# A gMLP layer's U and output products with the tokens stationary, its mixing by token, and DMA transposes for the blocks

## What is computed

```python
def gmlp_chunk_mixer(h, w_in, ln_g, ln_b, w_s, b_s, w_out):
    z = jax.nn.gelu(h @ w_in)
    u, v = jnp.split(z, 2, axis=-1)
    v = layer_norm(v, ln_g, ln_b)
    vc = v.reshape(B, S // CHUNK, CHUNK, GMLP_GROUPS, GMLP_GROUP)
    ws = jnp.where(causal[None], w_s, 0).astype(v.dtype)
    mixed = jnp.einsum('gts,bnsgc->bntgc', ws, vc) + b_s.T[None, None, :, :, None]
    return (u * mixed.reshape(B, S, GMLP_WIDTH)) @ w_out

def conv_ffn(h, w_gate, w_up, conv_w, conv_b, w_down):
    g = causal_dwconv3(h @ w_gate) + conv_b
    return (jax.nn.silu(g) * (h @ w_up)) @ w_down

for i in range(2):
    h = h + mixer_i(rms_norm(h, ...))
    h = h + conv_ffn(rms_norm(h, ffn_ln[i]), ...)
return rms_norm(h, final_ln)
```

## Time and profile before

| | us |
|---|---|
| median of 3 runs (2198.03 to 2200.35) | 2198.29 |
| span of the profiled execution | 2196.6 |
| PE busy | 2187.2 (100%) |
| DVE busy | 1473.7 (67%) |
| ACT busy | 1152.3 (52%) |
| POOL busy | 62.0 (3%) |
| chain that ended last | PE 99% |
| U, from its first matmul to that of the output product | 94.52 to 190.63 |
| output product | 190.63 to 279.40 |
| F0 | 279.40 to 758.63 |

### The profile page before, as it was taken

How to read it: one execution, slowest core, us unless ns; L and a number is a source line. 1 busy time by engine, 2 the same in 40 slices (tenths; PEclk the granted TensorE clock), 3 DMA queues, 4 the chain that set the end, 5 groups by cost and what they waited for, 6 DMA issues and landing times.

```text
span 2196.6 us, 30226 instructions
## 1 busy us (share of the span) xinstructions
PE 2187.2 (100%) x10468; PEld 1845.2 (84%) x10468; DVE 1473.7 (67%) x1865; ACT 1152.3 (52%) x1476; POOL 62.0 (3%) x56
## 2 busy tenths in 40 slices
PE   9999999999999999999999999999999999999998
PEld 7888888888888888888888888888888888888887
DVE  7486757777776755555468888785767676775554
ACT  7554555555555544444456555555555555554443
POOL 0011100000000000001000000020000000000000
PEclk9999999999999999999999999999999999999999
DMA  7755567777777765555555656558776777786665
GB/s 280 250 174 172 191 208 220 213 220 213 223 214 219 213 201 196 190 188 204 192 184 182 201 180 196 170 185 218 213 223 209 225 209 221 214 243 204 201 199 165
DMA packets 243077, 451.55 MB, mean 206 GB/s; under 512 B 139888, under 2 KB 140016, under 8 KB 242352
## 3 DMA queue, kind: packets, MB, share of 16 engines
q1 hardware_dynamic: 231664, 442.28, 64.5%
q0 software_dynamic: 944, 6.03, 0.8%
q10 hardware_dynamic: 10384, 2.11, 0.5%
HBM read 419.38 MB, written 2.10 MB: 192 GB/s over the span
## 4 chain that ended last, share of the span: by engine, by line
PE 99%; DMA 0%; ACT 0%; DVE 0%; SPq 0%; ACTq 0%; issue 0%
PE acc L1535 25%; PE acc L1537 25%; PE acc L1536 25%; PE acc L1513 14%; PE acc L1514 8%; PE sc_ps L1535 0%; PE sc_ps L1537 0%; PE sc_ps L1536 0%; PE sc_ps L1755 0%; DMA raw<-w_stream 0%; PE acc L1845 0%; PE acc L1663 0%; PE acc L1661 0%; PE acc L1662 0%; PE misc L1786 0%; PE sc_ps L1786 0%
## 5 line engine op out<-in xcount | busy, mean ns | idle before, releaser
L1039 DVE TENSOR_TENSOR w_lo<-raw,w_hi 128x1024 fp32r<-128x1024 f32 x782 | 962.9, 1234 | 612.3 <-ACT w_hi L655 611.3
L655 ACT ACTIVATE w_hi<-raw 128x1024 fp32r<-128x1024 f32 x782 | 828.6, 1062 | 730.3 <-PE acc L1537 603.4
L1535 PE MATMUL acc<-w_hi,X 128*128 128x512 f32 x1688 | 658.1, 390 | 0.0
L1537 PE MATMUL acc<-w_lo,X 128*128 128x512 f32 x1688 | 657.4, 389 | 0.0
L1536 PE MATMUL acc<-w_hi,X 128*128 128x512 f32 x1688 | 657.2, 389 | 0.0
L1537 PEld LDWEIGHTS acc<-w_lo,X 128*128 128x128 f32 x1688 | 317.0, 188 | 65.8
L1536 PEld LDWEIGHTS acc<-w_hi,X 128*128 128x128 f32 x1688 | 317.0, 188 | 65.5
L1535 PEld LDWEIGHTS acc<-w_hi,X 128*128 128x128 f32 x1688 | 317.0, 188 | 65.3
L1513 PE MATMUL acc<-X,w_hi 128*128 128x512 f32 x1024 | 359.2, 393 | 0.0
L1514 PE MATMUL acc<-X,w_lo 128*128 128x256 f32 x1024 | 288.7, 282 | 0.0
L1535 PE MATMUL acc<-w_hi,hid 128*128 128x512 f32 x688 | 268.1, 390 | 0.0
(11 more groups left out here) (211 smaller groups left out, 1350.6 us busy)
## 6 DMA issues: line engine op xcount, KB each, us to landing
raw<-w_stream SPq DMA_DIRECT2D x782, 512.0 KB, 3.9
h<-x_t SPq DMA_DIRECT2D x8, 256.0 KB, 6.1
out<-Z SPq DMA_DIRECT2D x4, 512.0 KB, 3.0
f_turned_a<-hc SPq DMA_TRANSPOSE x88, 3.2
f_turned_a<-tsum SPq DMA_TRANSPOSE x88, 3.2
std_rinv<-hc SPq DMA_TRANSPOSE x88, 4.1
std_rinv<-tsum SPq DMA_TRANSPOSE x88, 3.6
raw<-w_stream SPq DMA_DIRECT2D x4, 256.0 KB, 3.9
```

Source lines behind the costliest of these rows:

```text
L655: nc.scalar.activation(placed(w_hi, slot, exact(c, rounds)), raw[slot][:, :], ACT.Copy).then_inc(hi_ready, 1)
L1039: nc.vector.tensor_tensor(placed(w_lo, slot, at), raw[slot][:, :], placed(w_hi, slot, at), ALU.subtract)\
L1535: nc.tensor.matmul(bank, xh, hi, start=(kt == 0), stop=False)
L1537: op = nc.tensor.matmul(bank, xh, lo, start=False, stop=(kt == k_tiles - 1))
```

## The change

- **U and the output product** use `token_unit`, in blocks of 512 features, eight units each. The output product's units go in the order `AO_SPLIT`: six of block 0, four of block 1, the rest of 0, the rest of 1, then blocks 2 and 3. Weights are laid out to match; `by_depth` goes.
- **U's result**: ACT takes the gelu straight out of PSUM with the token's scale (`u_evac`), for a block at step 8, 16, 24 and 32.
- **Mixing** is done with `WS` stationary and both chunks of V as 256 columns: one matmul a group, four groups behind units 12, 16, 21 and 28. DVE adds the bias and multiplies with U in one instruction a group (`gate`). POOL has no part in it.
- **Turning**: U x mixed, the output product and D0's first three blocks have tokens on the partitions and are turned as F0 turns its results, in one helper: DVE cuts two planes (`cut_rows`), SP issues four DMA transposes of 128x4x128 (`turn_rows`), DVE puts the halves together (`set_rows`). For U the steps of cutting and setting are `U_CUT_AT` and `U_SET_AT`; in the products setting comes two steps after cutting (`SET_AFTER`), the addition to `h` one step later, `x_low` one and two steps after that. The output product and D0 are cut straight from PSUM. D0's last block is still turned on PE.
- `mean_square(0)` and its root and reciprocal go. `token_mean_square(1)` comes one unit later.

```diff
+MIX_AT = {12: 0, 16: 1, 21: 2, 28: 3}
+U_GATE_AT = (16, 19, 25, 32)
+U_CUT_AT = (17, 21, 26, 32)
+U_SET_AT = (20, 24, 29, 34)
+AO_SPLIT = ((0, range(6)), (1, range(4)), (0, range(6, 8)), (1, range(4, 8)), (2, range(8)), (3, range(8)))
+AO_ORDER = [(c, n) for c, ns in AO_SPLIT for n in ns]
+AO_DONE = [1 + max(u for u, (b, _) in enumerate(AO_ORDER) if b == c) for c in range(BLOCKS)]
+SET_AFTER = 2
...
 @block.sync
+            def turn_rows(n):
+                for r in range(2):
+                    sp.wait_ge(row_cut, 2 * n + r + 1)
+                    wait_pos(sp, row_set, 2 * n)
+                    for t in range(2):
+                        sp.dma_start(row_planes[r][:, :, P * t:P * (t + 1)],
+                                     turned_planes[r][:, t, :].rearrange("p (g f) -> p g f", g=4),
+                                     transpose=True).then_inc(row_landed, 16)
...
+            ahead = AHEAD + RING
+            at = loads_and_turns(OPENING, [(R_U + c, U_U + U_CUT_AT[c] + ahead) for c in range(BLOCKS)] +
+                                 [(R_AO + c, U_AO + AO_DONE[c] + ahead) for c in range(BLOCKS)])
...
 @block.gpsimd
-            for j in range(KT // 2 - 1):
-                pool.wait_ge(gelued, P_U + j + 1)
-                pool.wait_ge(mix_ready, 2 * j + 2)
-                nc.gpsimd.tensor_tensor(by_chunk(U[:, 2 * j:2 * j + 2, :]), by_chunk(U[:, 2 * j:2 * j + 2, :]),
-                                        mixed_pair(j), ALU.mult).then_inc(gated, 1)
...
 @block.scalar
+            def u_evac(c):
+                act.wait_ge(units_done, U_U + BLOCK_UNITS * (c + 1))
+                act.wait_ge(tok_rinv_ready, 1)
+                for t in range(2):
+                    nc.scalar.activation(U[:, t, COLS * c:COLS * (c + 1)], acc[c % 2][:, t, :], ACT.Gelu_apprx_tanh,
+                                         scale=tok_rinv[:, t:t + 1]).then_inc(gelued, 1)
+            def gx_high(c):
+                act.wait_ge(row_set, 2 * (R_U + c + 1))
+                act.wait_ge(v_normed, 2 * BLOCKS)
+                for b in range(2):
+                    nc.scalar.activation(GX[:, pair_of(2 * c + b), 0:S], feats_of(R_U + c)[:, pair_of(b), :], ACT.Copy)\
+                        .then_inc(gx_hi, 1)
...
             for k in range(4, KT * KT // UT + 4):
                 split_step(U_U, k)
-                gelu_evac(P_U + j, j, k % 4, j % 2, U, U_U + 4 * (j + 1))
+                if k % BLOCK_UNITS == 0:
+                    u_evac(k // BLOCK_UNITS - 1)
+                if k in U_SET_AT:
+                    gx_high(U_SET_AT.index(k))
...
+            for s in range(4, BLOCKS * BLOCK_UNITS + 4):
                 split_step(U_AO, s)
+                for c in range(BLOCKS):
+                    at = s - AO_DONE[c] - SET_AFTER - 1
+                    if at in (0, 1):
+                        residual(1, P_AO + 2 * c + at, 2 * c + at)
...
 @block.vector
+            def cut_rows(n, source):
+                if n:
+                    dve.wait_ge(row_landed, ROW_TURNS * n)
+                for r in range(2):
+                    nc.vector.tensor_copy(turned_planes[r], source(r)).then_inc(row_cut, 1)
+            def set_rows(n):
+                dve.wait_ge(row_landed, ROW_TURNS * (n + 1))
+                for r in range(2):
+                    nc.vector.tensor_copy(feats_plane(n, r), row_planes[r]).then_inc(row_set, 1)
+            def product_rows(norm, n, pd, c, done, k):
+                if k == 0:
+                    dve.wait_ge(units_done, done)
+                    cut_rows(n, lambda r: acc_plane(c % 2, r))
+                if k == SET_AFTER:
+                    set_rows(n)
+                if k == SET_AFTER + 1:
+                    add_rows(n, pd, c)
+                if k - SET_AFTER - 2 in (0, 1):
+                    pr = 2 * c + k - SET_AFTER - 2
+                    dve.wait_ge(pair_summed, pd + pr + 1)
+                    x_low(norm, pr)
...
+            def gate(c):
+                dve.wait_ge(mixed, c + 1)
+                dve.wait_ge(gelued, 2 * (c + 1))
+                for g in range(4 * c, 4 * (c + 1)):
+                    at = U[:, :, P * g:P * (g + 1)]
+                    nc.vector.scalar_tensor_tensor(at, mix_of(g), ws_bias[:, g:g + 1], at, ALU.add, ALU.mult)\
+                        .then_inc(gated, 1)
...
 @block.tensor
-                    wait_pos(pe, pair_summed, P_U + k // 4 - 1)
-                multiply(U_U + k, k % RING, tiles_of(k // 4 % 2, X, KT, k % 4))
+                token_unit(U_U + k, k % RING, acc[c % 2], X, 2 * n, KT)
+                if k in MIX_AT:
+                    mix(MIX_AT[k])
...
-            product(U_AO, P_AO, KT // 2, GX, KT, gx_needed, deep=True)
+            for k, (c, n) in enumerate(AO_ORDER):
+                if n == 0 and c < 2:
+                    pe.wait_ge(gelued, 2 * (c + 3))
+                elif n == 0:
+                    pe.wait_ge(row_cut, 2 * (R_AO + c - 1))
+                token_unit(U_AO + k, k % RING, acc[c % 2], GX, 2 * n, KT, gx_needed if c == 0 else None)
```

More of the change, by code:

```diff
@@ L261, in trunk @@
         WS = place("WS", at, [P, KT, P])
-        BS = place("BS", at + 8 * BLK, [P, KT, P])
+        row_feats = [place(f"row_feats{i}", at + (8 + 4 * i) * BLK, [P, 4, S]) for i in range(2)]
         v_junk = place("v_junk", 2 * KT * BLK, [P, D // 2])
@@ L283, in trunk @@
         at += 4 * SC * 4
-        down_tok = [nc.alloc_sbuf_tensor_at(f"down_tok{i}", [P, 2, COLS], F32, offset=x_at + (12 + 2 * i) * row)
-                    for i in range(2)] + [place("down_tok2", at - 4 * SC * 4, [P, 2, COLS])]
+        down_tok = place("down_tok", at - 4 * SC * 4, [P, 2, COLS])
+        down_feats = [nc.alloc_sbuf_tensor_at(f"down_feats{i}", [P, 4, S], F32, offset=x_at + (12 + 2 * i) * row)
+                      for i in range(2)]
         nmax = place("nmax", at, [P, 2])
@@ L538, in turn_head, with loads_and_turns @@
                                  transpose=True).then_inc(p_landed[h_ % 2], 16)
+            def turn_rows(n):
[6 more added lines that the diff above has]
+                                     transpose=True).then_inc(row_landed, 16)
+            def loads_and_turns(at, turns):
+                for n, u in turns:
+                    if at < (u + 1) // RING * RING:
+                        loads(at, (u + 1) // RING * RING)
+                    for v in range((u + 1) // RING * RING, u + 1):
+                        next_unit(v)
+                    turn_rows(n)
+                    at = -(-(u + 1) // RING) * RING
+                    for v in range(u + 1, at):
+                        next_unit(v)
+                return at
             def f_block(layer, u0, b):
@@ L660, in settled @@
                 act.wait_ge(vecs_landed, 16)
-            def high_copy(pair, s, done):
-                act.wait_ge(units_done, done)
-                nc.scalar.activation(hc[:, :, :], acc[s][:, :, 0:S], ACT.Copy).then_inc(hcopied, 1)
             def square_pair(n, pr):
@@ L1614, in f_block @@
             def f_block(layer, u0, b, i=0, before=None):
-                if before is None:
+                if before is not None and layer == 0:
+                    pe.wait_ge(row_cut, 2 * (R_AO + 3 + b))
+                elif before is None:
                     pe.wait_ge(f_evacuated, 4 * i + (F_CUTS * layer + 2 * (b - 1)))
@@ L1623, in f_block @@
                                normed_ready(1 + 2 * layer) if before is not None and b == 0 else None, kind=u0)
-                    if before is not None and b == 0 and n == 5:
+                    if before is not None and b == 0 and n == 6 - layer:
                         token_mean_square(1 + 2 * layer, lambda t: ssum[:, P * t:P * (t + 1)])
@@ L1904, in stream @@
     first = by_tokens(w_in[KT:]).reshape(BLOCKS, BLOCK_UNITS, UT, P, P)
[L1905 removed]
+    u_half = by_tokens(w_in[:KT])
+    w_out = by_tokens(blocks(a_w_out)).reshape(BLOCKS, BLOCK_UNITS, UT, P, P)
+    parts = [np.stack([first[c, n] for c, n in V_ORDER]), u_half, np.stack([w_out[c, n] for c, n in AO_ORDER]), by_tokens(ffn[0].reshape(-1, KT, P, P)), by_tokens(blocks(down[0])),
              v[:-1], qk.reshape(-1, P, E), v[-1:], blocks(b_w_o), by_tokens(ffn[1].reshape(-1, KT, P, P)), by_tokens(blocks(down[1]))]
```

289 lines of the change are left out of this document (113 added, 176 removed).

## The result

The changed kernel takes 2201.14 us (median of 21 runs, 2199.83 to 2204.06) against 2198.48 for the kernel before (21 runs beside them): a ratio of 1.0013, 95% interval 1.0007 to 1.0019. It is slightly slower, by 2.7 us, where 2.5 us faster was forecast, and lies just above the range. The profiled execution spans 2199.4 us; the median stands 1.7 us above it, as before.

The account below looks back on a forecast made before the run. PE was taken to set the time, by its own work and by late split units. 7.0 us less PE work minus 4.5 of stalls gave 2.5 us faster, 2195.8 us; range 2191.0 to 2201.0.

Parts of the forecast that it names:

- PE's own work, 7.0 us: PE saves 3.5 by the token form, 2.7 by 24 fewer transposes, 0.4 by one mean square, 0.4 by mixing.
- the form: U and output product: token form takes 2.720 us a unit against 2.774, saving 3.5 us over 64 units.
- mixing: U: 16 mixing matmuls of 256 columns replace 32 of 128 columns, saving 0.4 us on PE.
- the mean square: One mean square on PE goes, saving 0.4 us.
- The cut from PSUM: DVE's copy from PSUM, absent from the earlier trace: bounds 0.68 and 1.23 us, taken as 1.2.
- The landing: The last of a turn's four DMA transposes lands 2.5 us after its own start.
- the rival of late landing: Transposes share DMA engines with weights and land at 4.1 us; stalls 12.1, time 2203.4 us; chance 0.15.
- a landing over 3: Sign of being wrong: a turn's last transpose landing more than 3 us behind its start.
- The stalls, 4.5 us: PE waits for split units behind turns: 1.6 us at place A plus 2.9 at place B.
- Place A: End of U: the turn of its last block makes PE stand 1.6 us before the output product's unit 5.
- Place B: Output product: block 1's turn meets block 0's; PE waits 1.2 us at unit 21, 1.7 at unit 22, 2.9 together.
- Elsewhere nothing: Turns that come alone, F0's unit 6 (X wanted at 16.3, ready at 15.6) and U's blocks 0 to 2: no PE wait.

Follow-up runs that it names:

- e2: Changed kernel without the four DMA transposes of each turn; rows are set from the cut planes unturned, all other work stays: 2191.23 us, ratio 0.9968.
- e1: Kernel before, with only D0's first three blocks turned by DMA transposes: 2195.87 us against 2198.53, ratio 0.9989.
- e8: Changed kernel with POOL's additions of the squares behind the output product cut from 512 columns to 2: 2199.0 us, ratio 1.0003.
- e4: Changed kernel with U's last block set two steps later and the output product's first two blocks ended after 10 and 16 units: 2197.6 us, ratio 0.9996.
- e9: Changed kernel with U's last block set two steps later and output product blocks 0 to 2 set three steps behind their cut: 2191.73 us, ratio 0.9971.
- e11: Changed kernel with only output product blocks 0 to 2 set three steps after their cut instead of two: 2197.02 us, ratio 0.9992.
- e12: Changed kernel with SP's four transposes of U's last block moved ahead of two loads: 2202.83 us, ratio 1.002.
- e7: Changed kernel with one more DMA transpose in each of the 11 turns, into a spare buffer: 2212.14 us, ratio 1.0062.
- e10: e9 with the output product's last block turned on PE instead of by DMA: 2192.21 us, ratio 0.9973.

## Why the prediction was wrong

**What bounds the kernel** held: PE by its own work, and by split units that come late.

**PE's own work, 7.0 us: right, term by term.** e2, without any wait, has a span 6.9 below that of before. The output product falls from 88.77 to 87.04, which is the 32 x 0.054 forecast, and in both stages together the form is worth what F0's rate said. D0 alone gives 2.6 of 2.7 (e1). The output product starts 188.28 - 190.63 = 2.35 earlier; 1.7 of form, 0.4 of mixing and 0.4 of the mean square make 2.5, less 0.2 by which this profile's opening is longer (its first mean square starts at 42.10 instead of 41.91).

**The cut from PSUM: right.** 1.22 us from `acc` against 0.69 from U, both in 16-bit elements. The value taken from the fp32 row of the trace was the right one of the two. The Trainium skill ("VectorE: DVE Perf Modes", "Why PSUM operands drop a tier") caps a copy with an operand in PSUM at the one-port double mode, and the prediction read from this that a 16-bit copy could keep 0.68. But the same page ("Mode 2×_1P — pack two bf16 into one 32-bit read") gives that mode only to 16-bit elements at a step of one, and `acc_plane` takes every second 16-bit half. So the page too has the single mode here, and the trace agrees with it.

**The landing: right as a median, 2.5 us, and late where it counted once.** In nine of the eleven turns the last transpose landed 2.5 us behind its start, in place A too, so the rival of late landing doesn't explain places A and B. In two it landed late: 4.0 in U's block 1, where three steps cover it, and 3.7 in the output product's block 3, where it is half of F0's wait. The prediction named a landing over 3 as a sign of being wrong, and there it is.

**The stalls, 4.5 us: wrong, 9.5.** Three of its steps failed, and one term was missing.

1. *Place A, 1.6; it was 3.4.* The step "First cut: 4.05. Fourth transpose starts at 7.75, lands at 10.25" took 1.23 for each of four issues. The first pair took 3.80: 1.3 us, and the earlier trace rows had the row with the warning, a maximum of 2322 ns. The other 0.4 is DVE's late start at the gates, a split of the step before.
2. *Place B, 2.9; it was 3.7.* The chain was right within 0.3 us at each point, but the split was priced at 1.23 throughout (1.64 beside POOL's addition), ACT's 0.68 us wait between two pairs was left out, and unit 19, late by 0.2 on paper, was counted as nothing. With the first two gone (e8) 2.6 are left. The explanation that went with it, two turns that meet, was not the cause (e4): a lone turn empties the lead, and what follows it wins nothing back. The lead lasts where the set comes one step later (e9, e11), because DVE no longer stands in it, or because block 1's cut then no longer stands behind block 0's low parts; which of the two gives how much is open.
3. *"Elsewhere nothing": unit 31 0.2, F0 2.0.* For F0's unit 6 the sum had 0.7 us to spare, with the engines taken as on time. DVE came with three splits of debt (1.0), the last transpose landed 1.2 later than taken, and the wait was 1.55. In e11, without the debt and with a landing of 2.5, there is none. The token mean square waited for POOL's last sum, another 0.4. A margin below 1 us behind a stage that stalls is no margin.
4. *Missing: a first matmul behind a wait* takes 0.50 us instead of 0.39 to finish, and its successor starts 0.33 behind it instead of 0.23: 0.1 us for each of six waits, included in the numbers above.

The stalls add up: 3.4 + 3.7 + 0.2 + 0.2 (not resolved) in the output product and 2.0 in F0 are 9.5; less 7.0, and with the opening's 0.2, that is 2.7 of the 2.8 measured.

What was not weighed at all is the clock. In the changed kernel's profile it stays up behind the wait of place A; in e11 and e12, with waits of 2.8 and 3.6 us at the same place, it falls for some 3 us and costs 1.5. It may fall in some of the changed kernel's other runs as well. Nine of its 21 have a mean granted clock of 0.997 or 0.998, and their median is 2201.9 us against 2201.0 for the rest. The kernels that keep the wait of place A (changed, e7, e8, e11, e12) are below 0.999 in 29 of 57 runs. The kernel before and the variants without that wait (e1 to e4, e9, e10) are so in none of 120. By an estimate from e11 (3 us at half the clock in 2200) one such fall is 0.0007 of the mean, too near the last digit to count falls run by run.

## What to carry to other kernels

Where an engine waits for a DMA with urgent work queued behind the wait, place the wait by the longest issue and landing in the trace, not by the median, and look what else stands in a fixed order behind it: here three turns set one step later and one set two steps later, with no instruction saved, made a kernel 0.13% slower into one 0.29% faster. Price such a chain with the debt that the stage before hands over and with the work that follows the wait, since the lead comes back only if that work leaves room. Taking the latency out (e2) tells in one run how much there is to win.

## What the runs showed of the hardware

- **The clock after a wait.** PE's granted clock fell to 0.50 to 0.54 right behind waits of 2.8, 3.6 and 5.3 us, for some 3, 3 and 6 us, and the cost was 1.5, 1.5 and 2.7 us. Behind waits of 3.4 us in the changed kernel and 3.1 in e8 it stayed at 1.00, so the length of the wait alone doesn't decide. A wait of some microseconds in a busy PE can cost half as much again, and not each time.
- **The issue of a DMA transpose isn't constant.** 1.25 us is the median, 2.49 the maximum of the changed kernel, at the first transpose of U's last block; there it is long in every kernel that turns that block, and now and then at others. Loads ahead in the same queue are not the cause there (e12). Nor is the landing constant: 2.5 us behind the start of a turn's last transpose, but 4.0 and 3.7 in two turns of eleven.
- **DVE beside POOL.** The same split of 1024 elements takes 1.23 us, and 1.64 where a POOL addition of 512 elements (1.29 us, from 237.10) still runs in its first 0.56 us. What POOL's small work costs shows on DVE and not on POOL: some 2 us here (e8), together with ACT's wait.
- **A cut from PSUM.** Copying every second 16-bit half of 1024 fp32 words takes 1.22 us out of PSUM and 0.69 out of SBUF.
